# Hybrid mixer block: the eighth block of the scale's weights summed on TensorE, fillers counted by VectorE's sums, last token tile multiplied by its norm's weights ahead of the root

## What is computed

```python
mod = jax.nn.silu(c) @ w_ada[l] + b_ada[l]
sh1, sc1, g1, sh2, sc2, g2 = [m[:, None, :] for m in jnp.split(mod, N_MOD, axis=-1)]
h = _rmsnorm(x, norm_g[l, 0]) * (1.0 + sc1) + sh1
y = _mixer(h, ...)
x = x + g1 * _rmsnorm(y, norm_g[l, 1])
h = _rmsnorm(x, norm_g[l, 2]) * (1.0 + sc2) + sh2
y = (jax.nn.silu(h @ w_gate[l]) * (h @ w_up[l])) @ w_down[l]
x = x + g2 * _rmsnorm(y, norm_g[l, 3])
```

## Time and profile before

| | us |
|---|---|
| runs, median of 3 | 1685.34 (1685.32 to 1685.99) |
| the profiled execution, its own time | 1687.27 |
| its span, first to last instruction | 1685.5 |
| TensorE busy | 1644.5 |
| VectorE busy | 1047.9 |
| ScalarE busy | 610.9 |
| GpSimd busy | 821.5 |

### The profile page before, as it was taken

How to read it: one execution, slowest core, us unless ns; L and a number is a source line. 1 busy time by engine, 2 the same in 40 slices (tenths; PEclk the granted TensorE clock), 3 DMA queues, 4 the chain that set the end, 5 groups by cost and what they waited for, 6 DMA issues and landing times.

```text
span 1685.5 us, 23035 instructions
## 1 busy us (share of the span) xinstructions
PE 1644.5 (98%) x8072; PEld 1350.3 (80%) x8072; DVE 1047.9 (62%) x1766; ACT 610.9 (36%) x1153; POOL 821.5 (49%) x538
## 2 busy tenths in 40 slices
PE   6999999999999999999999999999999999999997
PEld 5777877778888888887888888888888888888886
DVE  7745885786999999366685347553354255345437
ACT  5543336482232222267224445223222213322323
POOL 2421131104356666520787135758556656755765
PEclk9999999999999999999999999999999999999999
DMA  9131131021111111412872330112012111201205
GB/s 352 38 86 40 53 104 45 32 70 32 47 47 47 47 47 44 157 53 88 300 247 90 131 125 26 63 50 75 25 50 75 50 50 50 68 31 50 75 27 211
DMA packets 37745, 138.90 MB, mean 82 GB/s; under 512 B 4656, under 2 KB 4784, under 8 KB 37680
## 3 DMA queue, kind: packets, MB, share of 16 engines
q1 hardware_dynamic: 35440, 130.70, 22.3%
q0 software_dynamic: 2240, 7.34, 1.9%
HBM read 118.10 MB, written 13.63 MB: 78 GB/s over the span
## 4 chain that ended last, share of the span: by engine, by line
PE 84%; DVE 7%; ACT 2%; DMA 2%; issue 2%; POOL 1%; DVEq 1%; SPq 0%; ACTq 0%; POOLq 0%
PE ps L716 25%; PE ps L718 25%; PE ps L717 25%; PE ps L963 2%; PE ps L927 2%; PE ps L845 1%; PE ps L846 1%; PE ps L747 1%; DVE region_c L2085 1%; DVE region_a L2258 1%; DVE region_a L2445 1%; DVE ps L2519 1%; DVE h_t L2077 0%; DMA region_b<-in_w_ada 0%; DVE region_b L2151 0%
## 5 line engine op out<-in xcount | busy, mean ns | idle before, releaser
L716 PE MATMUL ps<-h_t,w_t 128*128 128x512 f32 x1112 | 436.7, 393 | 3.0 <-DVE h_t L2077 2.5
L718 PE MATMUL ps<-h_t,w_t 128*128 128x512 f32 x1112 | 432.9, 389 | 0.0
L717 PE MATMUL ps<-h_t,w_t 128*128 128x512 f32 x1112 | 432.8, 389 | 0.0
L716 PEld LDWEIGHTS ps<-h_t,w_t 128*128 128x128 f32 x1112 | 208.8, 188 | 49.6 <-issue 5.3
L718 PEld LDWEIGHTS ps<-h_t,w_t 128*128 128x128 f32 x1112 | 208.7, 188 | 43.8
L717 PEld LDWEIGHTS ps<-h_t,w_t 128*128 128x128 f32 x1112 | 208.8, 188 | 43.0 <-issue 0.7
L1716 POOL TENSOR_TENSOR w_t<-raw,w_t 128x1280 fp32r<-128x1280 f32 (+1 forms) x50 | 142.8, 2856 | 194.8 <-ACT w_t L1275 194.4
L2460 DVE TENSOR_TENSOR y_f<-ps,y_f 128x512 f32<-128x512 f32 x120 | 80.8, 686 | 217.5 <-PE ps L718 217.5
L1876 POOL TENSOR_TENSOR w_t<-raw,w_t 128x512 fp32r<-128x512 f32 x80 | 109.8, 1377 | 138.0 <-ACT w_t L1604 138.0
L2131 DVE MAX8 top<-region_b 128x8 f32<-128x512 f32 (+5 forms) x192 | 159.2, 882 | 19.9 <-issue 19.1
L2134 DVE MATCH_REPLACE8 region_b<-top,region_b 128x512 f32<-128x512 f32 (+5 forms) x192 | 166.3, 876 | 0.0
(11 more groups left out here) (304 smaller groups left out, 3289.8 us busy)
## 6 DMA issues: line engine op xcount, KB each, us to landing
raw<-in_w_ffn SPq DMA_DIRECT2D x46, 512.0 KB, 4.0
raw<-in_w_gates SPq DMA_DIRECT2D x32, 640.0 KB, 3.9
region_b<-in_w_ada SPq DMA_DIRECT2D x33, 512.0 KB, 4.8
region_d<-in_w_ffn SPq DMA_DIRECT2D x20, 512.0 KB, 3.9
raw<-in_w_z SPq DMA_DIRECT2D x18, 512.0 KB, 3.4
region_a<-in_x SPq DMA_DIRECT2D x8, 512.0 KB, 14.9
h_f<-in_w_ada SPq DMA_DIRECT2D x8, 512.0 KB, 8.8
raw<-in_w_o SPq DMA_DIRECT2D x8, 512.0 KB, 3.6
```

Of the source, the lines that this page charges most:

```text
L716: pe.matmul(o, a_hi, m_hi, start=first, stop=False, skip_group_check=more)
L717: pe.matmul(o, a_hi, m_lo, start=False, stop=False, skip_group_check=more)
L718: return pe.matmul(o, a_lo, m_hi, start=False, stop=last, skip_group_check=more)
```

## The change

At the start, VectorE sums seven blocks instead of eight. The eighth is summed by TensorE: eight matmuls with the block itself as weights and the eighth column of silu(c) moving, which open bank 5, and onto which the column sums of the running sum are added. The seventh VectorE sum counts by two, so that the counts behind it stay as they were. The fillers are released by counts 2 to 5 of VectorE's sums, two calls at each.

At the end, for tile 7 alone: VectorE writes z plus the quarter back into `z` (in SBUF), and multiplies each half by its half of the norm's row into `y_gained`, a free place in `h_f`, before the root is known. `y_norm(6)` comes behind the first half of tile 7 instead of behind the second. ScalarE squares `z` instead of the banks. Behind the reciprocal, one pass per half multiplies `y_gained` by the reciprocal and adds x1.

```diff
+        y_gained = h_f[:, 0, 2]
...
-            def modulation(c, bank):
+            def modulation(c, bank, begun=False):
                 for k in range(KT):
                     mm = pe.matmul(ps[:, bank, k:k + 1], ada_sum1[:, c, k * P:(k + 1) * P], ones[:, 0:1],
-                                   start=True, stop=True)
+                                   start=not begun, stop=True, skip_group_check=begun)
                 mm.then_inc(s_mod, 1)
...
             turn_x(0)
-            for k in range(3, KT):
-                pe.wait_ge(s_scale_in[k], 16)
-                keep_busy(2 if k < 5 else 1)
+            for k in range(2, KT - 2):
+                pe.wait_ge(s_ada_used, k)
+                keep_busy(2)
+            pe.wait_ge(s_scale_in[KT - 1], 16)
+            for k in range(KT):
+                pe.matmul(ps[:, 5, k:k + 1], h_f[:, 0, KT - 1, k * P:(k + 1) * P], silu_c[:, KT - 1:KT],
+                          start=k == 0, stop=False, skip_group_check=True)
             pe.wait_ge(s_ada_used, KT)
-            modulation(1, 5)
+            modulation(1, 5, True)
             turn_x(1)
...
-                square_sum(last_pair(t), t, h_f[:, 0, t % 2])
+                square_sum(last_pair(t) if t < TT - 1 else z[:, t], t, h_f[:, 0, t % 2])
                 roots(t, t + 1, s_yroot)
...
-                weighted(ada_sum1[:, 1], h_f[:, 0, k], k).then_inc(s_ada_used, 1)
+                weighted(ada_sum1[:, 1], h_f[:, 0, k], k).then_inc(s_ada_used, 2 if k == KT - 2 else 1)
...
-            for k in range(KT):
+            for k in range(KT - 1):
                 scale_sum(k)
...
                     dve.wait_ge(s_y, i * 16 + (q + 1))
-                    dve.tensor_tensor(src if last else so_far, src, so_far, ALU.add).then_inc(s_yf, 1)
-                    if last and c and t >= 1:
+                    final = last and t == TT - 1
+                    dve.tensor_tensor(src if last and not final else so_far, src, so_far, ALU.add).then_inc(s_yf, 1)
+                    if final:
+                        dve.wait_ge(s_yf, i * 16 + (q + 1))
+                        dve.tensor_tensor(y_gained[:, c * HALF:(c + 1) * HALF], so_far,
+                                          g_row[1][:, c * HALF:(c + 1) * HALF], ALU.mult).then_inc(s_y_gain, 1)
+                    if last and c and 1 <= t < TT - 1:
+                        y_norm(t - 1)
+                    if final and c == 0:
                         y_norm(t - 1)
...
-            y_norm(TT - 1)
-            dve.wait_ge(s_y_norm, TT)
+            dve.wait_ge(s_yroot, TT)
+            order.then_wait(dve.reciprocal(rstd[:, TT - 1:TT], root[:, TT - 1:TT]))
+            dve.wait_ge(s_y_gain, 2)
             dve.wait_ge(s_x1_in[1], 64)
             for half in range(2):
                 c = slice(half * HALF, (half + 1) * HALF)
-                dve.tensor_tensor(x1[:, TT - 1, c], x1[:, TT - 1, c], z[:, TT - 1, c], ALU.add).then_inc(s_final_last, 1)
+                dve.scalar_tensor_tensor(x1[:, TT - 1, c], y_gained[:, c], rstd[:, TT - 1:TT], x1[:, TT - 1, c],
+                                         ALU.mult, ALU.add).then_inc(s_final_last, 1)
```

More of the change, by code:

```diff
@@ L443, in build @@
         s_y_norm = sem("s_y_norm")
+        s_y_gain = sem("s_y_gain")
         s_final = sem("s_final")
```

## The result

The changed kernel took 1692.16 us (median of 6 runs, 1691.58 to 1692.99), the kernel before, beside it, 1685.66 us: ratio 1.0035, 95% interval 1.0025 to 1.0045. Timed again beside other kernels (`both_again`) the ratio was 1.0027, interval 1.0016 to 1.0038. By these two ratios it is slower by 4.6 and 5.9 us; the medians themselves lie 6.5 us apart in the first measurement and 4.8 in the second. The forecast was 4.9 us, a ratio of 1.0029. The range ended at 1691.6 us: the ratio times the median of before that was shown, 1685.34, is 1691.2, inside it, while the 1692.16 itself lies 0.6 over it, in a measurement in which the kernel before also ran 0.3 higher.

A forecast was written before the change was run, and what follows sets the result against it. TensorE's matmuls were taken to bound the long middle, TensorE's path the start and VectorE the end. 2.37 us at the start plus 2.56 at the end made 4.9 us: 1690.3 us, 0.29% slower, range 1687.6 to 1691.6.

The forecast's parts named there:

- The fillers are never held by the counts: Start, TensorE: waits for counts 2 to 5 of VectorE's sums never hold the fillers, which run back to back.
- One filler call 0.68, eight one-column matmuls 1.69: Start, TensorE's path: these two additions sum to 2.37 us, putting the modulation columns at 26.0 instead of 23.63.
- VectorE's removed sum is worth nothing: Start, VectorE: removing one 1.37 us sum gains 0, since its next instruction waits for ScalarE's root anyway.
- The start shifts the whole program: Behind the modulation columns all engines go on from that one event, so everything shifts; bounds 0 and 2.37, taken 2.37 us.
- Rival 1: First 50 us: transfers absorb the later modulation, leaving only the end's +2.6 us, 1687.9 us; chance 14%.
- VectorE waits for GpSimd's whole instruction: End: two-SBUF-input products wait out GpSimd's adds, ending 0.55 us after them; last pass ends 2.56 us later.
- Rival 2: End: half speed beside GpSimd instead of a full stop, +0.87 us, with the start +3.2, 1688.6 us; chance 10%.
- rival 3: End: VectorE and GpSimd do not meet, products take 0.68 us; +0.13, in all +2.5, 1687.8 us; chance 8%.
- Behind it the stores cost what they cost now.: End: the stores behind the last pass take as long as before, so its +2.56 us counts in full.
- The sum: Whole kernel: 2.37 us at the start plus 2.56 at the end, 4.9 us slower.
- Rival 4: Start, TensorE: array falls back to 1.2 GHz during 32 one-column records; up to +1.8 us more, 1692.1 us; chance 8%.
- Rival 5: First tiles: seven collisions in VectorE's scaling of x go away, 6 us; with rival 3 1681.9 us, faster; chance 3%.

The follow-up runs named there:

- start_only: The kernel before with only the start's edits (modulation, fillers, eight matmuls, scale_sum), nothing of the end; ratio to the kernel before 1.0015.
- tail_late_norm: The kernel before with the end's edit alone, but y_norm(6) put back behind the last add, ahead of the second product; ratio to the kernel before 1.0019.
- tail_from_psum: The kernel before with y_norm(7) writing into its PSUM banks, where the two last adds read it; ratio to the kernel before 0.9999.
- tail_small_pool: The kernel before with the end's edit alone and GpSimd's adds of tiles 5 and 6 cut to 8 of 1024 columns; ratio to the kernel before 0.9993.
- start_few_fillers: The kernel before with the start's edit alone, but one filler call at each count instead of two; ratio to the kernel before 1.0007.

## Why the prediction was right, point by point

**The fillers are never held by the counts.** Right: 16 records back to back in every profile with this edit and two calls a count.

**One filler call 0.68, eight one-column matmuls 1.69.** The eight matmuls took 1.68. The fillers took 7.00 instead of 6.22 in the chain, 0.78, because the spacing fell to 0.34 us one record later than before (18.92 for 18.69, having started 0.4 us earlier). The column sums took 1.80 instead of 1.69, also in `start_only`, where the granted clock stayed at 1.00; why the second such group takes longer than the first is open. Together 2.57 for 2.37. It holds for this execution: where the fillers sped up early, in `start_only`, the columns were only 1.21 us later than before (11.08 for 9.87).

**VectorE's removed sum is worth nothing.** Right: it became 1.35 us more of idle time ahead of the root.

**The start shifts the whole program.** Right for the tile loop: 2.17 us at 24 us, 2.18 at 51 and still 2.13 at 161. Rival 1, absorption, is out; the start alone measured 1.0015. But the shift is not all that the edit costs: 0.8 us more come in the middle, at VectorE's pauses, a term that the sum had at nothing.

**VectorE waits for GpSimd's whole instruction.** Right, and it is what the forecast rested on at the end: products of 2.34 us, GpSimd's end plus 0.55. Rival 2 (half speed) would have given about 1.3 us, rival 3 0.7. Cutting GpSimd's adds to 8 columns gave 0.69 in the same places, which shows that GpSimd's adds are the cause; that the wait lasts to the end of the add is in the rows, by 0.55 us behind its end both times. In `tail_late_norm` the hold shows in the other direction. The Trainium skill (SBUF — State Buffer, section "SBUF: two separate sides") names both of these sides: two SBUF inputs make a VectorE instruction take part, and whoever starts first keeps the pair. The runs agree with both, by 2.34 and 0.69 us for the two-input product and 1.29 us for the two adds that read one input from PSUM.

**"Behind it the stores cost what they cost now."** This step failed, by 0.9 us. Before, the store of tile 6 (512 KB) was issued 0.55 us ahead of the last two, and these landed 2.8 us after issue. In the changed kernel it is issued 1.4 us ahead of them, and they land after 2.0 us. The other runs agree: 3.0 us where the last stores came 0.4 us behind GpSimd's add of tile 6 (`tail_from_psum`), 2.8 at 0.6 (`tail_late_norm`), 2.0 at 2.8 (`tail_small_pool`). So the end cost 1.8, not 2.6.

**The sum.** By the rows it is 2.57 for the start and 2.69 less 0.9 for the end, 4.4 us, and with the 0.8 in the middle 5.2, against measured ratios worth 4.6 and 5.9. That 4.9 came so near is in part luck: 0.9 too much for the stores stands against 0.8 that was left out and 0.3 by which start and tail were priced too low.

**Rival 4, the array falls back.** It happened, where I gave it 8%: granted 0.73 from 27 to 31 us. The mechanism was there, but its price was wrong. I added up to 1.8 us for slow fillers; they delayed the first token product (29.86, 4.1 us behind the modulation columns, against 2.4 before) and nothing else, since GpSimd's h pieces set the pace of that loop. That its 1692.1 us is almost the measured 1692.16 is chance.

**Rival 5, fewer collisions in the first tiles.** It did not happen: all engines kept their places against each other. Seven collisions were also too many: of the eight scalings of x four last 1.56 to 1.60 us, which makes some 3.4 us and not 6.

## What to carry to other kernels

Before work is moved ahead of a wait to hide it, look at what runs there on the engine that shares a port with it: here two products of 0.68 us became 2.34 us each, a loss of 1.65 us each, for one pass of 1.28 us that was gone behind the root. One operand in PSUM kept such a pass clear (1.29 us instead of 1.93 for two adds), but look first which other engine reads that bank at the time. And when a pass on one engine already hides behind another engine's work (y_norm(6) in the shadow of ScalarE's root), moving it out of there puts its full 1.4 us on the path. Last, a constant shift is not the whole price of an edit in front: compare the rows of the middle in several executions before calling a difference scatter.

## What the runs showed of the hardware that was not expected

- TensorE's granted clock fell to 0.50 (1.2 GHz) while the profile had it busy for all of the stretch (24 to 27 us in `start_few_fillers`), behind 32 records of one column each. It fell so in four of the five profiled executions with 32 such records; in `start_only` it stayed at 1.00, though these took 3.5 us there as in the changed kernel. With 16 such records it fell at this place in none of the six executions.
- The moment at which the filler spacing goes from 0.64 to 0.34 us differs between executions: 2.9 us after the first transpose in `start_only` (16.7 - 13.8), 4.9 before the change, 5.6 after it, about 6 in `start_few_fillers`. That alone is worth up to 1.4 us of this kernel's path. The kernel before feels little of it, since VectorE is ready at the same time: its start gave the columns 9.7 to 10.2 us after the first transpose in six executions, that of the changed kernel 11.1 to 12.4 in three. The Trainium skill (TensorE: Matmul & The Clock Gate, part 1 on the clock gate) says that the point varies from run to run; the variation here is larger than the half microsecond that it gives.
- The spacing of 0.64 us is that of the low clock: the fillers have it too where the granted clock reads 0.50 (26.5 to 30 us in `start_few_fillers`). That the view reads 1.00 on both sides of 18.69 in the earlier trace rows says nothing of the time ahead of it, since the trace's record of the granted clock begins only at 19.0 us.
- Two SBUF inputs are not the only case in which VectorE waits for GpSimd. The scaling of x (line 1990 before the change) reads and writes SBUF and has one such input; beside GpSimd's h pieces it lasts about 1.6 us instead of 0.75 and ends 0.55 us behind them (42.18 and 41.62; 48.54 and 48.00; 54.93 and 54.38). The passes that stayed clear here have one operand in PSUM.
- Single executions of the same middle part (161 to 939 us) drift by up to 1.5 us against each other, so a part of 1 us is read from its own rows and not from a span.
